# Two transformer blocks on one core: stationary width, buffers and order of products in the first attention

## The chip, the cores and the metric

One NeuronCore of a Trainium2 chip runs the whole program. The metric is the device time of one execution in microseconds, lower is better. A core has five engines with a queue each: TensorE (PE, matrix products; its weight loads are shown as PEld), VectorE (DVE), ScalarE (ACT), GpSimd (POOL) and SyncE (SP, which here issues the loads of weights).

## The reference

The input x has 512 positions of 1024 features. Two blocks are applied one after the other. What the change touches is all in the first one:

```python
proj = xn @ w_in[l]
pa, pb, pc, pd = jnp.split(proj, ...)
ya = short_conv_mixer(pa, w_sconv[l])
yb = dilated_mixer(pb, cos, sin)        # 4 heads of 64, windows with dilation
yc = forgetting_mixer(pc, b_forget[l])  # 4 heads of 64, causal, with a decay
yd = pool_mixer(pd, w_pool[l], pool_scale[l])
h = h + jnp.concatenate([ya, yb, yc, yd], axis=-1) @ w_out[l]
# memory_cross_attention: k and v of 256 memory rows
k, v = jnp.split(memn @ w_kv, 2, axis=-1)      # memn: rms_norm(mem)
```

Both mixers with heads are softmax attentions over four blocks of 128 queries. The rest (cross attention, gated feed-forward, spatial gating, differential attention, a second feed-forward) is the same before and after.

## The kernel before, in words

Activations lie as 8 chunks of 128 features x 512 positions. Each float32 operand of a large product is split into a high and a low part (ACT writes the high part, DVE subtracts it for the low one), and `product` (lines 431 to 435) issues three TensorE instructions for one: high x high, high x low, low x high. Weights come as units of 128 x 1024 floats, numbered through the program. SP loads a unit into one of two raw buffers (L398), ACT splits it (L992), DVE makes the low half (L1514), PE multiplies with it and counts it in `used`.

The stage of this case is **the first attention** (PE lines 597 to 703). It has 32 items: four groups g of two heads (group 0 and 2 dilated, 1 and 3 forgetting), and in each group four query blocks b and two heads h, so item t has group t // 8, block b = t % 8 // 2 and head h = t % 2. All engines walk through slots t = 0, 1, 2, ... in an order that is written out by hand:

- PE, slot t: `turn(t-3)` (transposes b+1 pieces of the probabilities into bank 2 or 3 of PSUM, L637), on even t `scores(t)` for both heads (L628, banks 0 and 1, 64 rows of the array each), in the first slots parts of the early output product and the gate's rows (L606), from slot 4 on `memory_half(t-4)`, and `weigh(t-5)`.
- ACT, slot t: `hi(t-4)` (high part of the turned probabilities, L1159), on t % 8 == 5 `output` (high part of the group's result, L1165), `exp(t-1)` (L1150), staging of the next group's q, k and v, `memory_out(t-4)`, with the split of a unit (L992) on even slots.
- DVE, slot t: `output`, `least(t)` (scores plus bias, and their minimum, L1742), `probs(t-2)` (L1749, L1751), `lo(t-4)` (L1757), staging (L1717, L1718), `memory_out(t-4)` (L1535 takes a key panel out of PSUM), and the low half of the unit (L1514).

`weigh(t)` multiplies the values with the turned probabilities: b+1 products, 3(b+1) instructions, with a stationary tile of 128 value columns, which are those of both heads; only the 64 rows of PSUM that belong to head h are used. The turned probabilities lie in two buffers (t % 2), so `hi(t)` waits for `weigh(t-2)`. The first `weigh` of a group waits until `output` has emptied banks 4 and 5 (semaphore mix_ready).

```python
if t % 8 == 0:
    pe.wait_ge(a1["v_staged"], t // 8 + 1)
    pe.wait_ge(early["added"], ADDED["w_out_early"] + KC)
    pe.wait_ge(mix_ready, 4 + t // 8)
...
def hi(t):
    act.wait_ge(a1["turned"], t + 1)
    if t >= 2:
        act.wait_ge(a1["pv"], t - 1)
```

`memory_half(t)` (lines 654 to 689) fills the waiting time: 16 units, each in two halves. Units m = 0 to 7 are key panels (24 instructions of 256 moving columns, into bank 6 or 7 by turns), units 8 to 15 are values (12 instructions of 512 columns), where a half takes one chunk k and both blocks of 128 memory rows, block 0 in bank 6 and block 1 in bank 7. After the first unit three column sums of squares go to bank 7 (L685, L687); ACT takes their root (L1179, L1180), DVE the reciprocals (L1778, L1779). Unit 1, which writes bank 7, waits for that root; unit 8 waits until both banks are empty of keys, unit 12 until ACT has taken block 0 of the values out of bank 6 (L1189).

After slot 36 the output product `into_residual("w_out", ...)` (L705) follows; its first column needs all eight chunks of the mixers' result (mix_ready 8).

## Time and profile before

| | us |
|---|---|
| median of 3 runs | 1979.04 (1977.53 to 1979.81) |
| time of the profiled execution | 1979.54 |
| its span, first to last instruction | 1977.7 |
| outside the span | 1.8 |
| the first attention, on the scale of the span | 141 to 285 |

The profile is of one execution. A row of a timeline gives the start and length of an instruction, its line, what it writes and reads, and in brackets how long its engine was idle before it and what ended that. PE's instructions overlap: what one costs in a full queue is the distance from its start to the next one's start, not its length. PEclk is the share of 2.4 GHz that was granted to TensorE, so 0.50 is 1.2 GHz.

### The profile page before, as it was taken

The numbers are of one execution on the slowest core, as the hardware profiler recorded it, in microseconds if no ns is written. First come the engines' busy times: TensorE is split into PE (matmuls) and PEld (weight loads), VectorE is DVE, ScalarE is ACT, GpSimd is POOL, SyncE is SP. The second block draws the span as 40 slices with busy tenths as digits, with TensorE's granted clock in tenths as the row PEclk, the third lists the DMA queues.
The fourth block names the chain that finished last, engine by engine and source line by source line (L and its number), as shares of the span: only waits on it lengthen the run. The fifth ranks groups of instructions, "written<-read, shape, count | busy, mean of one in ns | idle before, by whom it ended". The sixth has DMA issues, their size and how long they took to land.

```text
span 1977.7 us, 25235 instructions
## 1 busy us (share of the span) xinstructions
PE 1918.4 (97%) x8818; PEld 1565.4 (79%) x8818; DVE 1079.7 (55%) x1547; ACT 766.2 (39%) x1175; POOL 259.7 (13%) x206
## 2 busy tenths in 40 slices
PE   8998899899999999999999999999998999999998
PEld 6877778788787888888888888887775588888886
DVE  5866657567676624656644442255774364444323
ACT  4235455345545413453423232144554243323212
POOL 4702221020000001300100000023551020000001
PEclk9999999999999999998999999999996799999998
DMA  4222222122222322222222223222110122222222
GB/s 173 96 96 75 73 77 86 43 85 96 95 95 95 118 95 96 95 86 64 96 95 95 95 95 100 99 98 89 61 53 22 33 96 95 95 95 95 98 98 80
DMA packets 62331, 174.47 MB, mean 88 GB/s; under 512 B 5432, under 2 KB 23992, under 8 KB 62144
## 3 DMA queue, kind: packets, MB, share of 16 engines
q1 hardware_dynamic: 60912, 169.50, 25.5%
q10 hardware_dynamic: 1024, 2.94, 0.4%
q0 software_dynamic: 336, 1.25, 0.2%
q8 instruction: 37, 0.61, 0.1%
q14 instruction: 22, 0.18, 0.0%
HBM read 171.57 MB, written 2.10 MB: 88 GB/s over the span
## 4 chain that ended last, share of the span: by engine, by line
PE 91%; DVE 4%; ACT 2%; issue 1%; POOL 1%; DMA 1%; SPq 0%; DVEq 0%; ACTq 0%; POOLq 0%
PE ps L433 29%; PE ps L434 28%; PE ps L435 28%; PE ps L894 1%; PE ps L956 1%; PE ps L905 1%; POOL square_sum L2216 1%; DVE at_e L2148 1%; DMA w_raw<-in_weights 1%; DVE w_lo L1514 0%; PE ps L637 0%; PE ps L943 0%; PE ps L628 0%; DVE at_e L2132 0%; ACT w_hi L992 0%
## 5 line engine op out<-in xcount | busy, mean ns | idle before, releaser
L1514 DVE TENSOR_TENSOR w_lo<-w_raw,w_hi 128x1024 fp32r<-128x1024 f32 x302 | 379.3, 1256 | 494.5 <-ACT w_hi L992 494.1
L433 PE MATMUL ps<-xg_hi,w_hi 128*128 128x512 f32 (+1 forms) x1448 | 565.8, 391 | 13.9 <-DVE w_lo L1514 10.1
L434 PE MATMUL ps<-xg_lo,w_hi 128*128 128x512 f32 (+1 forms) x1448 | 558.9, 386 | 0.0
L435 PE MATMUL ps<-xg_hi,w_lo 128*128 128x512 f32 (+1 forms) x1448 | 558.7, 386 | 0.0
L992 ACT ACTIVATE w_hi<-w_raw 128x1024 fp32r<-128x1024 f32 x302 | 318.0, 1053 | 558.6 <-PE ps L435 553.0
L433 PEld LDWEIGHTS ps<-xg_hi,w_hi 128*128 128x128 f32 x1448 | 273.7, 189 | 80.3 <-DVE w_lo L1514 17.1
L435 PEld LDWEIGHTS ps<-xg_hi,w_lo 128*128 128x128 f32 x1448 | 273.6, 189 | 54.8
L434 PEld LDWEIGHTS ps<-xg_lo,w_hi 128*128 128x128 f32 x1448 | 273.8, 189 | 53.6 <-issue 1.0
L433 PE MATMUL ps<-hid_hi,w_hi 128*128 (+1 forms) x528 | 205.5, 389 | 0.0
L434 PE MATMUL ps<-hid_lo,w_hi 128*128 (+1 forms) x528 | 205.4, 389 | 0.0
L435 PE MATMUL ps<-hid_hi,w_lo 128*128 (+1 forms) x528 | 205.4, 389 | 0.0
L2213 POOL COPY square_sum<-squares 128x512 f32<-128x512 f32 x7 | 4.8, 689 | 1010.5 <-ACT squares L1007 1003.0
L433 PEld LDWEIGHTS ps<-hid_hi,w_hi 128*128 128x128 f32 x528 | 99.1, 188 | 20.9 <-DVE w_lo L1514 0.4
L435 PEld LDWEIGHTS ps<-hid_hi,w_lo 128*128 128x128 f32 x528 | 99.1, 188 | 20.7
L434 PEld LDWEIGHTS ps<-hid_lo,w_hi 128*128 128x128 f32 x528 | 99.1, 188 | 20.4
L2216 POOL TENSOR_TENSOR square_sum<-square_sum,squares 128x512 f32<-128x512 f32 x49 | 78.3, 1598 | 61.3 <-ACT squares L1007 60.3
L433 PE MATMUL ps<-w_hi,xg_hi 128*128 128x512 f32 x192 | 78.6, 409 | 3.4 <-DVE xa_k L1535 1.9
L435 PE MATMUL ps<-w_hi,xg_lo 128*128 128x512 f32 x192 | 76.0, 396 | 0.0
L434 PE MATMUL ps<-w_lo,xg_hi 128*128 128x512 f32 x192 | 76.0, 396 | 0.0
L1535 DVE TENSOR_TENSOR conv_a<-ps,r_cols 128x512 f32<-128x512 f32 x44 | 30.4, 691 | 78.5 <-PE ps L435 78.5
L1390 ACT ACTIVATE gate<-conv_g 128x512 f32<-128x512 f32 x44 | 27.8, 632 | 109.1 <-DVE conv_g L1535 109.1
L1520 DVE SCALAR_TENSOR_TENSOR xg_lo<-x,par,xg_hi 128x512 fp32r<-128x512 f32 x56 | 60.7, 1099 | 7.0 <-ACT xg_hi L1057 7.0
(323 smaller groups left out, 2599.2 us busy)
## 6 DMA issues: line engine op xcount, KB each, us to landing
w_raw<-in_weights SPq DMA_DIRECT2D x315, 512.0 KB, 3.2
out_cols<-result SPq DMA_DIRECT2D x8, 256.0 KB, 2.2
x<-in_x_cols SPq DMA_DIRECT2D x2, 512.0 KB, 5.2
x<-in_x_cols SPq DMA_DIRECT2D x1, 1024.0 KB, 8.4
squares<-in_mem_cols ACTq DMA_DIRECT2D x1, 512.0 KB, 3.8
sp_w<-in_spatial ACTq DMA_DIRECT2D x1, 512.0 KB, 4.1
sp_b<-in_spatial_bias ACTq DMA_DIRECT2D x1, 512.0 KB, 5.0
dil<-in_dil_table POOLq DMA_DIRECT2D x1, 448.0 KB, 9.3
```

The costliest lines, as they stand in the source:

```text
L433: nc.tensor.matmul(to, wh, xh, start=start, stop=False)
L434: nc.tensor.matmul(to, wh, xl, start=False, stop=False)
L435: return nc.tensor.matmul(to, wl, xh, start=False, stop=stop)
L894: mm = nc.tensor.matmul(ps[:, 2 * (n % 2) + h, 0:w], q_[rows, block_], k_[rows, 0:w], start=k == 0, stop=k == 2)
L905: mm = nc.tensor.transpose(ps[:, 4 + n % 2, j * P:(j + 1) * P], at3["e"][:, 2 * (n % DIFF_SLOTS), j * P:(j + 1) * P], ident)
L956: nc.tensor.matmul(ps[:, h % 4, :], pick, da["rms"], start=True, stop=True).then_inc(a3["spread"], 1)
L992: nc.scalar.activation(w_hi[:, u % 2, :], w_raw[:, u % 2, :], ACT.Copy).then_inc(w_hi_ready, 1)
L1390: nc.scalar.activation(ffn["gate"][:], ffn["tg"][:], ACT.Silu).then_inc(st["gated"], 1)
L1514: nc.vector.tensor_tensor(w_lo[:, u % 2, :], w_raw[:, u % 2, :], w_hi[:, u % 2, :].bitcast(F32), ALU.subtract).then_inc(w_ready, 1)
L1520: nc.vector.scalar_tensor_tensor(out=xg_lo[:, c, :], in0=x[:, c, :], scalar=column(gain, c), in1=xg_hi[:, c, :].bitcast(F32), op0=ALU.mult ...
L1535: return nc.vector.tensor_tensor(to, ps[:, bank, 0:cols], r_cols[:] if r is None else r, ALU.mult).then_inc(signal, 1)
L2216: nc.gpsimd.tensor_tensor(sums[:], sums[:], squares[:, c % 2, :], ALU.add).then_inc(summed, 1)
```

## The change

In the first attention alone:

- `weigh` takes only the 64 value columns of its own head as stationary columns, and both heads write rows 0 to 63 of their bank (4 or 5). ACT and DVE `output` read these rows and write the head's rows of the result. DVE's two parts each wait for ACT's part of the same head, where both waited for the second.
- Four buffers hold turned probabilities: the two of before and two more in memory that is free at that time. `hi(t)` now waits for `weigh(t-4)`.
- PE does no `weigh` in the slots with (t-5) % 8 of 0 and 1; on t % 8 == 7 it does three, items t-7, t-6 and t-5.
- DVE does `lo(t-4)` first in a slot, ahead of `output`, `least` and `probs`.
- The memory's sums of squares go to bank 5; `weigh(1)` waits for the root in place of unit 1, and PE waits ahead of the sums until the early output sums have left bank 5.
- The halves of value units are by block: the first half does both chunks k for block 0 (bank 6), the second for block 1 (bank 7). Unit 8's first half waits for 7 key panels, its second for 8; unit 12's halves wait for one block of values each; ACT takes block 0 out after the first half of the unit before.

```diff
--- before.py
+++ after.py
@@ -230,8 +230,7 @@
 
 
         at1 = dict(e=sb("at1_e", [P, 3, S], F32, m_ctx), least=sb("at1_least", [P, 3], F32, m_ctx),
-                   sums=sb("at1_sums", [P, 3], F32, m_ctx), inv=sb("at1_inv", [P, 3], F32, m_ctx),
-                   pt_hi=xg_hi[:, 4:6, :], pt_lo=xg_lo[:, 4:6, :])
+                   sums=sb("at1_sums", [P, 3], F32, m_ctx), inv=sb("at1_inv", [P, 3], F32, m_ctx))
         sb("at1_to_line", [P, LINE // 4], F32, m_ctx)
         for set_ in range(2):
             for part in ("qhi", "qlo", "khi", "klo"):
@@ -239,6 +238,14 @@
             at1[f"vhi{set_}"] = xg_hi[:, 6 + set_, :]
             at1[f"vlo{set_}"] = xg_lo[:, 6 + set_, :]
         m_ctx.close()
+
+        def turned_probs(t):
+
+            if t // 2 % 2 == 0:
+                return xg_hi[:, 4 + t % 2, :], xg_lo[:, 4 + t % 2, :]
+            if t // 8 < 2 * GC - 1:
+                return mix["hi"][:, KC - 2 + t % 2, :], mix["lo"][:, KC - 2 + t % 2, :]
+            return (at1["khi0"], at1["klo0"]) if t % 2 else (at1["qhi0"], at1["qlo0"])
 
         def mem_split(to, c):
 
@@ -339,7 +346,7 @@
                    "turned", "pt_hi", "pt", "pv", "out", "bias", "sq", "summed", "rms", "spread", "normed", "out_hi",
                    "out_lo")
         lams = stage("lambda", "dots", "exps", "done")
-        mem = stage("mem", "hi", "lo", "sq", "summed", "sums", "rms", "r", "k_ready", "v_ready")
+        mem = stage("mem", "hi", "lo", "sq", "summed", "sums", "rms", "r", "k_ready", "values", "v_ready")
         xqs = stage("xq", "ready")
         ffn_stages = {"up": stage("up", "scaled", "tapped", "steps", "gated", "product", "hid_hi", "hid", "zero"),
                       "gu": stage("gu", "scaled", "gated", "product", "hid_hi", "hid")}
@@ -640,15 +647,19 @@
             def weigh(t):
                 b, h = t % 8 // 2, t % 2
                 pe.wait_ge(a1["pt"], t + 1)
+                if t == 1:
+                    pe.wait_ge(mem["rms"], 2)
                 if t % 8 == 0:
                     pe.wait_ge(a1["v_staged"], t // 8 + 1)
                     pe.wait_ge(early["added"], ADDED["w_out_early"] + KC)
                     pe.wait_ge(mix_ready, 4 + t // 8)
                 vh, vl = group_buffers(t, ("vhi", "vlo"))
+                turned_hi, turned_lo = turned_probs(t)
                 for j in range(b + 1):
                     cols = slice(j * P, (j + 1) * P)
-                    mm = product(ps[:, 4 + h, b * P:(b + 1) * P], vh[:, cols], vl[:, cols],
-                                 at1["pt_hi"][:, t % 2, cols], at1["pt_lo"][:, t % 2, cols], j == 0, j == b)
+                    own = slice(j * P + HD * h, j * P + HD * h + HD)
+                    mm = product(ps[0:HD, 4 + h, b * P:(b + 1) * P], vh[:, own], vl[:, own],
+                                 turned_hi[:, cols], turned_lo[:, cols], j == 0, j == b)
                 mm.then_inc(a1["pv"], 1)
 
             def memory_half(t):
@@ -659,32 +670,32 @@
                     if m == 0:
                         pe.wait_ge(mem["lo"], KC)
                         pe.wait_ge(gate["rows"], 1 + N_FORGET)
-                    if m == 1:
-                        pe.wait_ge(mem["rms"], 2)
                     if 2 <= m < KC:
                         pe.wait_ge(mem["k_ready"], m - 1)
-                    if m == KC:
-                        pe.wait_ge(mem["k_ready"], KC)
-                    if m == KC + 4:
-                        pe.wait_ge(mem["v_ready"], MB)
+                if m == KC:
+                    pe.wait_ge(mem["k_ready"], KC - 1 + half)
+                if m == KC + 4:
+                    pe.wait_ge(mem["v_ready"], 1 + half)
                 if m < KC:
                     for k in range(KC // 2 * half, KC // 2 * (half + 1)):
                         wh, wl = tile(u % 2, k)
                         mm = product(ps[:, 6 + m % 2, 0:M], wh, wl, mem_split(xg_hi, k), mem_split(xg_lo, k), k == 0, k == KC - 1)
                 else:
-                    k = 2 * (m % 4) + half
-                    cols = slice(half * S, (half + 1) * S)
-                    for b in range(MB):
-                        block_ = slice(b * P, (b + 1) * P)
-                        mm = product(ps[:, 6 + b, :], mem_split(xg_hi, k)[:, block_], mem_split(xg_lo, k)[:, block_],
+                    block_ = slice(half * P, (half + 1) * P)
+                    for k in (2 * (m % 4), 2 * (m % 4) + 1):
+                        cols = slice(k % 2 * S, (k % 2 + 1) * S)
+                        mm = product(ps[:, 6 + half, :], mem_split(xg_hi, k)[:, block_], mem_split(xg_lo, k)[:, block_],
                                      w_hi[:, u % 2, cols], w_lo[:, u % 2, cols], k == 0, k == KC - 1)
                 if half:
                     mm.then_inc(used, 1)
+                elif m in (KC + 3, KC + 7):
+                    mm.then_inc(mem["values"], 1)
                 if t == 1:
                     pe.wait_ge(mem["summed"], KC)
-                    nc.tensor.matmul(ps[:, 7, 0:M], ones, memory["acc"][:], start=True, stop=True)
+                    pe.wait_ge(early["added"], ADDED["w_out_early"] + KC)
+                    nc.tensor.matmul(ps[:, 5, 0:M], ones, memory["acc"][:], start=True, stop=True)
                     for b in range(MB):
-                        mm = nc.tensor.matmul(ps[:, 7, M + b:M + b + 1], memory["acc"][:, b * P:(b + 1) * P], ones[:, 0:1],
+                        mm = nc.tensor.matmul(ps[:, 5, M + b:M + b + 1], memory["acc"][:, b * P:(b + 1) * P], ones[:, 0:1],
                                               start=True, stop=True)
                     mm.then_inc(mem["sums"], 1)
 
@@ -699,7 +710,10 @@
                     early_unit(t + 1)
                 if 0 <= t - MEM_LAG < 4 * KC:
                     memory_half(t - MEM_LAG)
-                if t >= 5:
+                if t >= 5 and (t - 5) % 8 >= 2:
+                    if t % 8 == 7:
+                        weigh(t - 7)
+                        weigh(t - 6)
                     weigh(t - 5)
 
             into_residual("w_out", KC, 0, mix["hi"], mix["lo"], mix_ready, lambda k: k + 1,
@@ -1153,16 +1167,16 @@
 
             def hi(t):
                 act.wait_ge(a1["turned"], t + 1)
-                if t >= 2:
-                    act.wait_ge(a1["pv"], t - 1)
+                if t >= 4:
+                    act.wait_ge(a1["pv"], t - 3)
                 w = P * (t % 8 // 2 + 1)
-                nc.scalar.activation(at1["pt_hi"][:, t % 2, 0:w], ps[:, 2 + t % 2, 0:w], ACT.Copy).then_inc(a1["pt_hi"], 1)
+                nc.scalar.activation(turned_probs(t)[0][:, 0:w], ps[:, 2 + t % 2, 0:w], ACT.Copy).then_inc(a1["pt_hi"], 1)
 
             def output(g):
                 act.wait_ge(a1["pv"], 8 * (g + 1))
                 for h in range(2):
                     rows = slice(HD * h, HD * h + HD)
-                    nc.scalar.activation(mix["hi"][rows, 4 + g, :], ps[rows, 4 + h, :], ACT.Copy).then_inc(a1["out_hi"], 1)
+                    nc.scalar.activation(mix["hi"][rows, 4 + g, :], ps[0:HD, 4 + h, :], ACT.Copy).then_inc(a1["out_hi"], 1)
 
             def memory_in(c):
                 if c == 0:
@@ -1176,16 +1190,19 @@
 
                 if t == 2:
                     act.wait_ge(mem["sums"], 1)
-                    nc.scalar.activation(memory["rms"][:], ps[:, 7, 0:M], ACT.Sqrt, bias=column("eps"), scale=1.0 / D).then_inc(mem["rms"], 1)
-                    nc.scalar.activation(memory["rms_rows"][:], ps[:, 7, M:M + MB], ACT.Sqrt, bias=column("eps"),
+                    nc.scalar.activation(memory["rms"][:], ps[:, 5, 0:M], ACT.Sqrt, bias=column("eps"), scale=1.0 / D).then_inc(mem["rms"], 1)
+                    nc.scalar.activation(memory["rms_rows"][:], ps[:, 5, M:M + MB], ACT.Sqrt, bias=column("eps"),
                                          scale=1.0 / D).then_inc(mem["rms"], 1)
                 m = t // 2 - 1
                 if t % 2 == 0 and 0 <= m < 2 * KC:
                     if m in (KC + 3, KC + 7):
                         h = (m - KC) // 4
-                        act.wait_ge(used, FIRST["mem_k"] + m + 1)
                         act.wait_ge(mem["r"], 2)
                         for b in range(MB):
+                            if b == 0:
+                                act.wait_ge(mem["values"], h + 1)
+                            else:
+                                act.wait_ge(used, FIRST["mem_k"] + m + 1)
                             nc.scalar.activation(xa["v"][:, b, h * S:(h + 1) * S], ps[:, 6 + b, :], ACT.Copy,
                                                  scale=memory["r_rows"][:, b:b + 1]).then_inc(mem["v_ready"], 1)
                     split(FIRST["mem_k"] + m + 2)
@@ -1754,14 +1771,15 @@
             def lo(t):
                 w = P * (t % 8 // 2 + 1)
                 dve.wait_ge(a1["pt_hi"], t + 1)
-                nc.vector.tensor_tensor(at1["pt_lo"][:, t % 2, 0:w], ps[:, 2 + t % 2, 0:w],
-                                        at1["pt_hi"][:, t % 2, 0:w].bitcast(F32), ALU.subtract).then_inc(a1["pt"], 1)
+                turned_hi, turned_lo = turned_probs(t)
+                nc.vector.tensor_tensor(turned_lo[:, 0:w], ps[:, 2 + t % 2, 0:w], turned_hi[:, 0:w].bitcast(F32),
+                                        ALU.subtract).then_inc(a1["pt"], 1)
 
             def output(g):
-                dve.wait_ge(a1["out_hi"], 2 * g + 2)
                 for h in range(2):
+                    dve.wait_ge(a1["out_hi"], 2 * g + h + 1)
                     rows = slice(HD * h, HD * h + HD)
-                    ins = nc.vector.tensor_tensor(mix["lo"][rows, 4 + g, :], ps[rows, 4 + h, :], mix["hi"][rows, 4 + g, :].bitcast(F32),
+                    ins = nc.vector.tensor_tensor(mix["lo"][rows, 4 + g, :], ps[0:HD, 4 + h, :], mix["hi"][rows, 4 + g, :].bitcast(F32),
                                                   ALU.subtract)
                 ins.then_inc(mix_ready, 1)
 
@@ -1790,14 +1808,14 @@
             for j in range(2):
                 early_sum("w_out_early", j, MIX_EARLY_BANKS[j])
             for t in range(MIX_ITEMS + 6):
+                if 0 <= t - 4 < MIX_ITEMS:
+                    lo(t - 4)
                 if t % 8 == 5 and t > 8:
                     output(t // 8 - 1)
                 if t < MIX_ITEMS:
                     least(t)
                 if 0 <= t - 2 < MIX_ITEMS:
                     probs(t - 2)
-                if 0 <= t - 4 < MIX_ITEMS:
-                    lo(t - 4)
                 g = t // 8 + 1
                 if t % 8 == 1 and g < 2 * GC:
                     stage_qk(g)
```

## Rows read from the trace of the kernel before

**Rows 1.** The page: the chain that ended last, its shares by engine.

```profile
PE 91%; DVE 4%; ACT 2%; issue 1%; POOL 1%; DMA 1%; SPq 0%; DVEq 0%; ACTq 0%; POOLq 0%
```

**Rows 2.** Windows: length, busy time of PE, PEld, DVE, ACT, POOL, PEclk, DMA share, GB/s.

```profile
182.10:199.40 17.30, 17.30 (x151) 16.39 (x150) 12.72 (x33) 9.02 (x22) 7.64 (x10) 1.00 0.20 67
...
226.50:233.30 6.80, 6.80 (x24) 5.54 (x22) 1.58 (x3) 2.05 (x5) 0.00 (x0) 0.50 0.24 77
...
264.00:267.50 3.50, 3.50 (x13) 2.89 (x12) 2.66 (x6) 0.09 (x1) 0.00 (x0) 0.51 0.00 0
...
141.00:285.00 144.00, 128.02 (x804) 107.42 (x803) 92.20 (x223) 74.74 (x162) 32.40 (x40) 0.94 0.23 75
```

**Rows 3.** Timeline, PE alone: start, length, instruction, idle time before it and who ended it.

```profile
176.30 0.55 PE L433 MATMUL ps<-xg_hi,w_hi 128*128 128x256 f32 x1 [2.53 <-ACT mem_rms_rows L1180]
...
202.49 0.30 PE L433 MATMUL ps<-xg_hi 128*128 128x128 f32 x1 [1.36 <-DVE mix_lo L1764]
...
203.75 0.41 PE L637 MATMUL ps<-con,at_e 128*128 128x128 f32 x2 [0.74 <-DVE xg_lo L1757]
...
210.47 0.52 PE L637 MATMUL ps<-con,at_e 128*128 128x128 f32 x3 [0.96 <-DVE xg_lo L1757]
...
225.74 0.47 PE L433 MATMUL ps<-w_hi,xg_hi 128*128 128x512 f32 x1 [1.88 <-DVE xa_k L1535]
...
255.60 0.47 PE L433 MATMUL ps<-w_hi,xg_hi 128*128 128x512 f32 x1 [1.30 <-ACT xa_v L1189]
...
284.62 0.50 PE L433 MATMUL ps<-mix_hi,w_hi 128*128 128x512 f32 x1 [0.57 <-DVE mix_lo L1764]
```

**Rows 4.** Timeline, PE: inside a weighing at the granted clock 1.00, then in one at 0.50.

```profile
185.58 0.22 PE L433 MATMUL ps<-xg_hi 128*128 128x128 f32 x1
185.64 0.28 PE L434 MATMUL ps<-xg_lo,xg_hi 128*128 128x128 f32 x1
185.76 0.27 PE L435 MATMUL ps<-xg_hi,xg_lo 128*128 128x128 f32 x1
...
179.11 0.41 PE L434 MATMUL ps<-xg_lo,xg_hi 128*128 128x128 f32 x1
179.32 0.41 PE L435 MATMUL ps<-xg_hi,xg_lo 128*128 128x128 f32 x1
```

**Rows 5.** Groups of weight loads over the span, 128 and 8 columns: mean ns behind the comma.

```profile
L453 PEld LDWEIGHTS ps<-square_sum,con 128*128 128x128 f32 x14 | 2.6, 188 | 1.5 <-issue 1.0
...
L943 PEld LDWEIGHTS ps<-squares,con 128*8 128x8 f32 x16 | 0.9, 88 | 2.9 <-ACT squares L1485 1.6 <-issue 0.9
```

**Rows 6.** Timeline, PE, differential attention: weighing, two products with 8 stationary columns, weighing.

```profile
1529.33 0.27 PE L435 MATMUL ps<-at_pt_hi,at_v_lo 128*128 128x128 f32 x1
1529.53 1.02 PE L943 MATMUL ps<-squares,con 128*8 128x512 f32 x2
1530.49 0.33 PE L433 MATMUL ps<-at_pt_hi,at_v_hi 128*128 128x128 f32 x1
1530.65 0.27 PE L434 MATMUL ps<-at_pt_lo,at_v_hi 128*128 128x128 f32 x1
```

**Rows 7.** Timelines of ACT, DVE and PE around the memory's root.

```profile
174.23 1.28 ACT L1179 ACT_TABLE_LOAD   x1
...
176.19 1.75 DVE L1778 RECIPROCAL mem_r_cols<-mem_rms 128x256 f32<-128x256 f32 x1
...
180.43 0.69 DVE L1742 CUSTOM_DVE_ANT_0 at_e<-ps,dil 128x512 f32<-128x512 f32 x1 [0.88 <-PE ps L637]
...
183.11 0.52 PE L637 MATMUL ps<-con,at_e 128*128 128x128 f32 x3
```

**Rows 8.** Timelines of ACT and of DVE at the first change of group.

```profile
199.72 1.20 ACT L1165 ACTIVATE mix_hi<-ps 64x512 fp32r<-64x512 f32 x2
...
200.96 1.39 DVE L1764 TENSOR_TENSOR mix_lo<-ps,mix_hi 64x512 fp32r<-64x512 f32 x2 [1.25 <-ACT mix_hi L1165]
...
205.23 0.69 DVE L1742 CUSTOM_DVE_ANT_0 at_e<-ps,proj 128x512 f32<-128x512 f32 x1 [1.62 <-PE ps L628]
```

## The prediction

> **What bounds the kernel now.** I read the chain that ended last first: TensorE is 91% of it [rows 1], so an edit pays only where it shortens PE's own work or a wait of PE. Then windows over the first attention [rows 2]: of 144.0 us between 141 and 285 PE is busy 128.0, so about 16 us are waits. Within a group it doesn't wait at all (17.30 of 17.30 us from 182.1 on), while the granted clock falls to 0.50 from 226.5 to 233.3, to 0.51 in 264.0 to 267.5, and once more after 175. Last, the waits one by one in PE's timeline [rows 3]. Seven are to be seen: 2.53 us for the memory's root, three at the first change of group (1.36, 0.74, 0.96), 1.88 for the eighth key panel, 1.30 for the first half of the values, 0.57 ahead of the output product. The other two changes of group repeat the pattern of the first (0.03, 0.74, 0.68 and 1.43, 0.74). That is 13 us; the other 3 lie in the first slots and stay. The stage is bound by PE inside a group, and by the ACT-DVE chain at its seams and at the memory's root. About 0.2% (4 us) is what a measurement of this kernel can tell from no change.
>
> **Part 1, narrow weighing.** There are 240 instructions, in 32 blocks of n = 3, 6, 9, 12. A full-width one costs 0.12 to 0.11 us from start to start; the one whose load had been done in advance cost 0.06 (185.58 to 185.64) [rows 4]. So 128 moving columns need 0.06, and the load of 128 stationary columns sets the pace. Loads take 188 ns at 128 columns and 88 at 8, that is 0.83 ns a column [rows 5]; 64 columns fewer save 0.053. The pace inside a block should fall from 0.112 to 0.065, by 0.047 for each of its n-1 further instructions.
>
> Against that stands the change of width. Before shows none at 64 columns; the nearest rows are the products with 8 columns between weighings [rows 6]. Going in, the interval is 0.20 in place of 0.11: 0.09 more. Coming out, the second interval is 0.16 (1530.49 to 1530.65) in place of 0.11, 0.05 more, and the first I price like the way in, 0.09. The first narrow product, whose successor's load can't be done ahead, takes 0.11 in place of 0.06: 0.05. Together a block pays 0.09 + 0.05 + 0.09 + 0.05 = 0.28 (0.29 unrounded), and its gain is 0.047(n-1) - 0.29: -0.19, -0.05, 0.09, 0.23 for the four sizes. The first three blocks of a group are now one of 12 instructions: 0.35 + 11 x 0.065 = 1.06, against 3 x 0.06 + 9 x 0.112 = 1.19, so 0.13. A group saves 0.13 - 0.05 + 2 x 0.09 + 2 x 0.23 = 0.72, four save 2.9; some 0.4 falls where DVE sets the pace: **2.5 us**. Bounds: if a change of width costs nothing, 208 x 0.047 = 9.8, some 8 of it where PE sets the pace; if loads don't get shorter and the switch stays, 24 x 0.29 = -7. I take the middle, since both prices have a row of the same kind.
>
> The Trainium skill ("TensorEngine Tiling (Array Packing)", Key Properties) says that a change of tiling mode drains TensorE. The trace agrees (0.20 in place of 0.11 where the width changes), and the page gives no price. The skill ("TensorE: Matmul & The Clock Gate", Back-to-back issue gap) gives about 81 ns for sustained pairs of load and product at 128 columns. The trace has 112 at full width and differs; with 81 as the narrow pace, by that page alone, this part would come to about -0.6 us.
>
> **Part 2, sums in bank 5.** PE loses its 2.53 us wait, but what is late next is DVE. The sums end at 172.2. ACT no longer waits for `weigh(0)` with `hi(2)`, so its table load of 1.28 [rows 7] starts then, at 172.25 instead of 174.23, and the root is there at 174.1. DVE is the late one. It was free for the reciprocal at 176.1; scores(6), for which it waited before that, come 0.36 earlier (3 x 0.12, as `weigh(0)` is gone from ahead of them), and `lo(2)` (0.34) is done before, so it is free at 175.4. The reciprocal (1.75, at 176.19 before) starts 0.8 earlier. The key panel and the unit's low half follow, then least(7), which had waited 0.88 for PE at the low clock: 180.43 - 0.8 - 0.88 = 178.75, plus lo(3) 0.34 = 179.1. least (0.69) and probs (0.5) follow and turn(5) starts at about 180.5, where it was 183.11: **2.6 us**, the low clock of that place included. PE has turn(4) at 175.2, half a unit (12 x 0.12) and the three weighings (1.1) until then, gets there at 178 and stands for 2.5 us: nearly the same wait, at another instruction. The added wait for early sums is covered, since PE at that point has already waited for DVE's later slot 4. `weigh(1)`'s wait for the root finds it done (174.1 against 177).
>
> **Part 3, value units by block.** Unit 8's first half needs the seventh panel only, out two slots earlier: the 1.88 goes. Its second half comes a slot later and finds the eighth done, which was so by 225.7 even then. Unit 12's first half still waits for ACT's copy of block 0. DVE and ACT reach this place when they did, so half of the 1.30 is my estimate of what stays, between none and all. **2.5 us.** ACT could take block 0 earlier, but it stands behind exp in its queue, so I count no more.
>
> **Part 4, four buffers, weighing put off, `lo` first.** At a change of group count from R = 199.55, when weigh(7) is done (0.17 ahead of ACT's first copy; `hi(9)` lies between). Before, turn(11) starts at R+4.2 and turn(13) at R+10.9 [rows 3]. ACT's two copies take 1.20 and DVE's two subtractions 1.39, starting after the second copy (200.96) [rows 8]. Now `hi(9)` is out of the way, DVE starts after the first copy, at R+0.63, and `lo` doesn't stand behind least and probs: turn(11) at about R+3.3. PE has only half a unit to do there (1.5 us) and waits 1.7: the 1.36 turns up again at turn(11). From least(14) to turn(13) it was 5.24 (205.23 to 210.47); with lo(10) ahead of it, 4.9. least(14) starts 1.48 behind turn(11), so turn(13) starts at R+9.7, with weighings 8 to 10 done as before: 1.2 us. The second change gives 1.0; at the third, without staging behind it, 0.5. **2.7 us**, not the 6.7 that the waits add up to. `hi(8g+12)` now waits for the first of the three weighings; hi, lo and turn behind it have a slot of time. The last output gives **0.6** [rows 3]: DVE's first subtraction runs beside ACT's second copy.
>
> **Part 5, the clock.** A weighing instruction takes 0.21 at 0.50 against 0.11 [rows 4]. In 226.5 to R2 = 230.5, the end of weigh(15) and PE-bound, that cost 1.8 (12 x 0.1 for it and 3 x 0.2 for products of 512 columns); after 264.0, 1.6. The first of these follows the 1.88 wait, which goes, the second a wait that is moved. Both back: **3.4**. But waits of 2.5 and three times 1.7 stand in the new order, as long as those after which the clock fell, and some will be followed by a low stretch. One of 6.8 us costs 6.8 x (1 - 0.112/0.213) = 3.2; I charge one, **-3.0**.
>
> **Sum**: 2.5 + 2.6 + 2.5 + 2.7 + 0.6 + 3.4 - 3.0 = 11.3. The profiled execution took 1979.5 (span 1977.7 and 1.8 around it), so 1968.2; the median of the runs is 0.5 below it: 1967.7. Behind the stage nothing changes, and the weight stream has room (DMA share 0.23 over the stage) [rows 2].
>
> **The rivals.**
> - *The forecast*, gain 7 to 15: 0.48.
> - *Cheap switches, no low clock*: 14.3 + (8 - 2.5) = 19.8, so 1959.2. For it: 64 columns is not 8, and the products of 8 columns are of another kind. Against: the waits that stay. Gains over 15: 0.21.
> - *Waits moved and the clock falls at two or three seams*: 14.3 - 3 x 3.2 = 4.7, so 1974.3. For it: the seams keep 1.7 us waits. Against: the first change of group had 1.36 and 0.96 and the clock stayed. Gains of 4 to 7: 0.17.
> - *The narrowing doesn't do what it says* (loads not shorter, switch in full): 11.3 - 2.5 - 7 = 1.8, so 1977.2, within 0.2%: 0.08.
> - *Slower*: half-width products leave TensorE looking idle, and the clock stays low in the weighing slots through the stage. Each 6.8 us stretch costs 3.2, so past the 14.3 it takes five, and from six of them (41 of the 100 us) it is over 1979.0 by 5: 1984. For it: the stage's granted clock is 0.94 even now [rows 2]. Against: weighing is 240 instructions of over 800, and full-width units stand in every slot. 0.06.
>
> Faster 0.86, same 0.08, slower 0.06. The range takes the price of the switch from near zero to full, and no to three low stretches: 1959.5 to 1975.
>
> **What would show it.** Weighing groups of 80 instructions with 64 columns at some 0.065 start to start, and 0.20 at the first of a block (part 1). No wait at unit 1, but some 2.5 us at turn(5) for DVE (part 2); no wait at unit 8, 0.6 at unit 12 (part 3); waits of 1.7 at turn(11), (19), (27) on DVE in place of the weighing's (part 4); one low stretch in the stage. It would be wrong if these waits are gone or longer, if the pace inside a block stays 0.11, or if the clock is low throughout.

## The result, and the profile after

The changed kernel takes 1957.11 us (median of four runs, 1956.26 to 1957.49) against 1979.42 for the one before (1977.53 to 1982.03): ratio 0.9886, interval 0.9869 to 0.9903. It is 22.3 us faster. The sign was forecast, the size was not: 11.3 us were, and the time lies below the range.

The profiled execution took 1957.36, with a span of 1955.5. I measure the stage from the first scores to the first product of the cross attention's queries. That is 163.03 us before (141.44 to 304.47) and 145.45 after, so **17.6 us are gained in the stage and 5.2 behind it**, in work that is the same instruction by instruction. Ahead of the stage 0.6 are lost: the first scores start at 142.06 instead of 141.44. Windows of both kernels, columns as in [rows 2]. Of the changed kernel: the stage, the rest, two stretches of low clock in the stage (a third begins at 166.7) and the longest one behind it. Below them, of the kernel before: the stage, the rest and the longest stretch. All three stretches of low clock in the stage come to 13.65 us after, and to 17.07 before.

```profile
142.06:287.51 145.45, 133.59 (x888) 109.38 (x888) 108.40 (x238) 86.88 (x179) 42.33 (x46) 0.95 0.25 82
287.51:1955.50 1667.99, 1634.97 (x7375) 1333.24 (x7373) 876.58 (x1202) 633.42 (x938) 158.90 (x110) 0.98 0.26 87
...
180.30:187.10 6.80, 6.12 (x32) 5.67 (x33) 3.94 (x12) 3.67 (x8) 2.20 (x2) 0.50 0.31 110
248.60:252.00 3.40, 3.40 (x12) 2.27 (x12) 1.64 (x5) 1.82 (x4) 0.87 (x2) 0.50 0.00 0
1474.00:1504.72 30.72, 24.32 (x100) 18.03 (x100) 17.11 (x52) 15.92 (x43) 6.47 (x5) 0.50 0.06 18
```

```profile
141.44:304.47 163.03, 147.05 (x887) 123.44 (x887) 106.79 (x238) 86.01 (x179) 41.03 (x46) 0.95 0.22 74
304.47:1977.70 1673.23, 1639.95 (x7375) 1336.77 (x7373) 876.45 (x1202) 633.33 (x938) 159.06 (x110) 0.97 0.26 86
1492.80:1526.93 34.13, 28.35 (x112) 20.25 (x112) 16.93 (x53) 16.66 (x45) 5.87 (x5) 0.50 0.05 16
```

PE was busy 147.05 us in the stage and is now 133.59, for the same number of instructions; the waits over 0.3 us fell less, from 15.9 to 11.8. So what went is mostly busy time of PE, less work and less low clock together. In the rest, 7375 instructions on both sides, 1673.23 became 1667.99, and the clock is the only thing that differs: the low stretch of the differential attention is 34.13 long before and 30.72 after, and the two after it, at 1540.6 and 1963.9, are shorter by 3.3 to 3.4 too.

The waits, in PE's timeline after, answer to [rows 3]:

```profile
180.98 0.90 PE L644 MATMUL ps<-con,at_e 128*128 128x128 f32 x3 [2.65 <-DVE at_e L1768]
...
201.25 0.44 PE L644 MATMUL ps<-con,at_e 128*128 128x128 f32 x2 [1.79 <-DVE at_e L1768]
...
207.59 0.55 PE L644 MATMUL ps<-con,at_e 128*128 128x128 f32 x3 [0.85 <-DVE at_e L1768]
...
224.80 0.44 PE L644 MATMUL ps<-con,at_e 128*128 128x128 f32 x2 [1.54 <-DVE at_e L1768]
...
248.17 0.44 PE L644 MATMUL ps<-con,at_e 128*128 128x128 f32 x2 [1.86 <-DVE at_e L1768]
...
267.63 0.50 PE L440 MATMUL ps<-mix_hi,w_hi 128*128 128x512 f32 x1 [0.70 <-DVE mix_lo L1782]
```

They stand where the prediction put them: 2.65 at turn(5), 1.79, 1.54 and 1.86 at turn(11), (19) and (27), all on DVE's probs (L1768); none at units 1, 8 and 12. Weigh(7) ends at 197.79 and ACT's first copy starts at 197.83. Set against that start, turn(11) comes at +3.4 and turn(13) at +9.8; forecast were +3.3 and +9.7.

What wasn't where it was put is the weighing. PE's timeline after: two rows of a block at the granted clock 0.50 (185.38), then a block of nine at 1.00 with the product ahead of it and the one behind it. Below it is the group of one of its weight loads:

```profile
185.38 0.31 PE L440 MATMUL ps<-mix_hi,xg_hi 128*64 128x128 f32 x1
185.48 0.31 PE L441 MATMUL ps<-mix_lo,xg_hi 128*64 128x128 f32 x1
...
188.34 0.28 PE L442 MATMUL ps<-xg_hi,w_lo 128*128 128x256 f32 x1
188.46 0.22 PE L440 MATMUL ps<-xg_hi 128*64 128x128 f32 x1
188.52 0.22 PE L441 MATMUL ps<-xg_lo,xg_hi 128*64 128x128 f32 x1
188.58 0.22 PE L442 MATMUL ps<-xg_hi,xg_lo 128*64 128x128 f32 x1
...
188.94 0.22 PE L442 MATMUL ps<-xg_hi,xg_lo 128*64 128x128 f32 x1
189.00 0.40 PE L644 MATMUL ps<-con,at_e 128*128 128x128 f32 x2
```

```profile
L442 PEld LDWEIGHTS ps<-xg_hi,xg_lo 128*64 128x64 f32 x32 | 4.3, 135 | 0.0
```

Inside a block the distance is 0.060, against 0.112 at full width [rows 4] (0.10 against 0.21 at the low clock). **Going in, it is 0.12 (188.34 to 188.46), what a product of 256 columns takes in front of its own kind; coming out, 0.06.** A change of width costs nothing here. Over all blocks behind a product of 256 columns, at the full clock, the interval going in is 0.117 to 0.122, and was 0.117 to 0.120 at full width; from the first transpose of a turn to its second it is 0.136, and was 0.134 (medians).

### The profile page after: what moved, and what is told of

The parts are those of the page before. It is cut to its first block, busy times and chain, and to the rows that moved or that the text cites. A ratio compares the mean times of both kernels' runs of the same rounds, so it can differ in the third digit from the quotient of the medians.

```text
span 1955.5 us, 25234 instructions
## 1 busy us (share of the span) xinstructions
PE 1899.1 (97%) x8818; PEld 1546.8 (79%) x8818; DVE 1081.4 (55%) x1547; ACT 767.2 (39%) x1175; POOL 260.8 (13%) x206
## 4 chain that ended last, share of the span: by engine, by line
PE 90%; DVE 5%; ACT 2%; issue 1%; POOL 1%; DMA 1%; SPq 0%; POOLq 0%; DVEq 0%; ACTq 0%
PE ps L440 29%; PE ps L441 28%; PE ps L442 28%; PE ps L908 1%; DVE w_lo L1531 1%; PE ps L970 1%; PE ps L919 1%; POOL square_sum L2234 1%; DMA w_raw<-in_weights 1%; DVE at_e L2166 1%; ACT w_hi L1006 0%; PE ps L635 0%; PE ps L644 0%; DVE at_e L1759 0%; PE ps L957 0%
## 5 line engine op out<-in xcount | busy, mean ns | idle before, releaser
L440 PE MATMUL ps<-xg_hi,w_hi 128*128 128x512 f32 (+1 forms) x1448 | 565.8, 391 | 12.6 <-DVE w_lo L1531 11.3
```

Of the source, the lines that this page charges most:

```text
L440: nc.tensor.matmul(to, wh, xh, start=start, stop=False)
```

## The experiments

Runs e1 to e12 stand each against the kernel before on the same chip; e1 to e4 share nine runs of it (1979.06, 1977.25 to 1983.29), e5 to e8 seven (1978.43, 1973.16 to 1981.35), e9 to e12 eleven (1977.22, 1973.43 to 1982.06). The changed kernel itself ran with another set, beside 1979.42. So a difference between one of these runs and the changed kernel is across sets, whose medians of the kernel before lie up to 2.2 us apart, and one of 1 or 2 us proves nothing by itself.

### e1 and e2: narrowing alone, and everything but it

e1 is the kernel before with the narrow `weigh` (and `output` reading rows 0 to 63); e2 is the changed kernel without both. The main lines of e2's edit:

```diff
-    mm = product(ps[0:HD, 4 + h, b * P:(b + 1) * P], vh[:, own], vl[:, own],
+    mm = product(ps[:, 4 + h, b * P:(b + 1) * P], vh[:, cols], vl[:, cols],
```

> The kernel before with the narrow weighing alone (64 stationary columns, rows 0 to 63 of the bank); two buffers, order, banks and halves as before. Theory A, the change of width costs nothing between 128 and 64 columns: the pace in a block is 0.06 and so is the first interval, 32 blocks save 208 x 0.05 = 10.6 us of PE time, some 8 to 10 of it in the time, about 1970, with the seven waits of before in place. Theory B, the one on record, a switch of 0.29 a block: 32 x 0.29 = 9.3 against 9.8, so no gain at all, about 1979.

> The changed kernel with 128 stationary columns again in the weighing, all else as changed. Theory A: slower than the changed kernel by 8 to 10 us, about 1966. Theory B: slower by 2.5, about 1960. The waits at turn(5), turn(11), turn(19), turn(27) stay at 2.6 and 1.5 to 1.9 either way.

e1: 1969.38 (1967.33 to 1976.04), ratio 0.9954, interval 0.9938 to 0.9969, 9.7 us faster than before. e2: 1963.51 (1962.12 to 1964.22), ratio 0.9919, 0.9902 to 0.9936, 6.4 slower than the changed kernel. So e1 is as its theory A had it (about 1970), and e2 lies between its theories (2.5 and 8 to 10 slower), nearer to A. The stage of e1, that of e2, and that of the changed kernel in a second profile (e15, below):

```profile
141.37:293.31 151.94, 131.41 (x887) 106.94 (x887) 106.25 (x238) 85.76 (x179) 40.90 (x46) 0.99 0.24 79
```

```profile
141.63:292.52 150.89, 142.05 (x887) 119.11 (x887) 108.77 (x238) 88.04 (x179) 42.35 (x46) 0.98 0.24 80
```

```profile
141.87:285.54 143.67, 131.01 (x888) 107.10 (x887) 108.41 (x238) 86.70 (x179) 42.37 (x46) 0.98 0.26 84
```

Narrowing was priced at 2.5 us, with 9.8 as its upper bound if a change of width is free. The stages differ by 11.1 us without the rest of the change (151.94 against 163.03) and by 5.4 with it (145.45 against 150.89), the times by 9.7 and 6.4. All are more than 2.5. The work alone is 208 x 0.052 = 10.8 us, at the full clock, and in both pairs part of it is waited for: PE's waits over 0.3 us grow from 15.9 to 19.7, and from 8.6 to 11.8.

What sets 11.1 and 5.4 apart is the clock, which these two comparisons don't hold equal. The stage has 17.07 us at the granted clock 0.50 in the kernel before and 3.41 in e1, but 6.83 in e2 and 13.65 in the changed kernel. In e15 the changed kernel has 6.83, as e2 has, and by its stage narrowing gives 7.2 (150.89 less 143.67). In e1, 13.66 us less of low clock are worth up to 7 of the 11.1 (an estimate: an instruction takes twice as long at 0.50). Whether narrowing itself makes the low stretches fewer isn't shown. **So narrowing gives more than was forecast, 5.4 to 7.2 us beside the rest of the change.**

### e3, e4 and e11: 32, 96 and 8 columns

The changed kernel with another width. 32 and 8 leave out values, 96 takes columns of the other head.

```diff
-    own = slice(j * P + HD * h, j * P + HD * h + HD)
-    mm = product(ps[0:HD, 4 + h, b * P:(b + 1) * P], vh[:, own], vl[:, own],
+    own = slice(j * P + HD * h, j * P + HD * h + 8)
+    mm = product(ps[0:8, 4 + h, b * P:(b + 1) * P], vh[:, own], vl[:, own],
```

> The changed kernel with 32 stationary columns in each weighing instruction; it leaves out the other 32 value columns of each head, so the attention's result is not computed in full. Theory A2, the switch costs only towards a quarter of the width (as the 8-column products showed): pace 0.06 as with 64, but 0.09 more at the first weighing of a block and some 0.15 more behind it, 24 x 0.24 = 5.8 us of PE time, 3 to 5 us slower. Theory A3, the 8-column products were slow for another reason: same time as the changed kernel.

> The changed kernel with 96 stationary columns (both heads take columns 0 to 95, so head 1 is computed wrongly). If the load sets the pace by 0.83 ns a column, the interval is 0.083 (64 columns: 0.06, 128: 0.11), so 240 x 0.023 = 5 us of PE time more, some 4 us slower. If the pace has two steps only, a full and a half width, it is 0.11 or 0.06 and the time that of the wide or of the narrow kernel.

> The changed kernel with 8 stationary columns in each weighing (most of the values are left out, to see the price of a change of width alone). Theory A (width has no price by itself; the 0.09 more at the products of 8 columns comes from what stands around them): pace about 0.06, entering interval 0.117 as with 64 and 32 columns, time 1957. Theory B (8 columns do cost a switch): 0.09 more going in and coming out, 32 blocks by 0.28, some 8 us less where DVE sets the pace: 1962 to 1966.

e3: 1957.23, ratio 0.989 (0.9874 to 0.9907); e4: 1960.92, 0.9907 (0.9891 to 0.9924); e11: 1956.95, 0.9889 (0.9864 to 0.9914). PE's timeline, from the last product ahead of the block on, in e11 and then in e4:

```profile
187.40 0.28 PE L442 MATMUL ps<-xg_hi,w_lo 128*128 128x256 f32 x1
187.52 0.22 PE L440 MATMUL ps<-xg_hi 128*8 128x128 f32 x1
187.58 0.22 PE L441 MATMUL ps<-xg_lo,xg_hi 128*8 128x128 f32 x1
187.64 0.23 PE L442 MATMUL ps<-xg_hi,xg_lo 128*8 128x128 f32 x1
```

```profile
187.68 0.28 PE L442 MATMUL ps<-xg_hi,w_lo 128*128 128x256 f32 x1
187.80 0.22 PE L440 MATMUL ps<-xg_hi 128*96 128x128 f32 x1
...
188.11 0.25 PE L441 MATMUL ps<-xg_lo,xg_hi 128*96 128x128 f32 x1
188.20 0.25 PE L442 MATMUL ps<-xg_hi,xg_lo 128*96 128x128 f32 x1
188.29 0.25 PE L440 MATMUL ps<-xg_hi 128*96 128x128 f32 x1
```

The pace is 0.06 at 8, 32 and 64 columns, 0.085 at 96 and 0.112 at 128. That was e4's first theory, and it came 3.8 us slower than the changed kernel, as forecast (some 4). From 128 to 96 it falls by 0.027, which is 0.84 ns a column, as the loads had it [rows 5]; below 64 nothing is gained, since the 128 moving columns need 0.06 anyway. The Trainium skill ("TensorE: Matmul & The Clock Gate", LDWEIGHTS) puts a load at its columns divided by 1.2, in ns. By that, an estimate, it is 107, 80 and 53 ns for 128, 96 and 64; the trace agrees within 5 ns for the first two (112 and 85) and for the third shows the 60 of the moving side.

Eight columns enter and leave like the others. So the 0.09 more at the differential attention's products of 8 columns [rows 6], on which the prediction's price hung, isn't a price of the width. Those products have 512 moving columns and other operands, and each waits for a semaphore of its own. They are of another kind too: two of them take 0.96 (1529.53 to 1530.49), where a product of 512 columns in the stage takes 0.23. The 512 columns alone don't cost it, since at two places in the stage before a weighing ahead of a product of 512 moving and 128 stationary columns takes 0.11 (from 277.56 and from 281.62 on). Which of the rest costs the 0.09 was not tried.

### e5 and e7: the bank and the buffers, each undone

e5 puts the sums back into bank 7, and unit 1 waits for the root. e7 has two turned buffers, a weighing in every slot and `hi(t)` behind `weigh(t-2)`, with `lo` first and bank 5 kept.

```diff
 # e5
-                if t == 1:
-                    pe.wait_ge(mem["rms"], 2)
...
+                    if m == 1:
+                        pe.wait_ge(mem["rms"], 2)
...
-                    nc.tensor.matmul(ps[:, 5, 0:M], ones, memory["acc"][:], start=True, stop=True)
+                    nc.tensor.matmul(ps[:, 7, 0:M], ones, memory["acc"][:], start=True, stop=True)
 # e7
-                if t >= 4:
-                    act.wait_ge(a1["pv"], t - 3)
+                if t >= 2:
+                    act.wait_ge(a1["pv"], t - 1)
...
-                if t >= 5 and (t - 5) % 8 >= 2:
-                    if t % 8 == 7:
-                        weigh(t - 7)
-                        weigh(t - 6)
+                if t >= 5:
                     weigh(t - 5)
```

> The changed kernel with the sums back in bank 7 (so that unit 1 waits for the root again); the four buffers stay. Theory A, the bank is not what brings the 2.6 us: ACT comes to its root early because hi(2) no longer waits for the first weighing, which is the buffers' work, and turn(5) hangs on DVE either way. Then turn(5) stays within 0.5 us of where it is (16.1 us after the first scores), TensorE waits about 1 us at unit 1 and that much less at turn(5), and the time is 1957 to 1958. Theory B, as the prediction had it (Part 2 is the bank's): turn(5) 2.6 us later, 1959.7. In both the clock can add or take some 3 us.

> The changed kernel with two turned buffers, a weighing in every slot and hi(t) behind weigh(t-2); lo stays ahead on DVE, sums stay in bank 5. Theory A (Part 4 as predicted, and Part 2's gain is the bank's): the weighings wait again at the three changes of group, turn(5) stays: 1959 to 1960. Theory B (the early root is the buffers' work): hi(2) stands behind the first weighing again, so the root comes about 2 us later and turn(5) with it, on top of the seams: 1961.5 to 1963.

e5: 1957.77 (1956.61 to 1957.91), ratio 0.9899 (0.988 to 0.9919). e7: 1960.44 (1958.45 to 1965.44), 0.992 (0.9895 to 0.9945). PE's timeline in e5, then in e7 (turn(5), and the first change of group):

```profile
175.40 0.36 PE L440 MATMUL ps<-xg_hi,w_hi 128*128 128x256 f32 x1 [0.58 <-ACT mem_rms_rows L1193]
...
181.63 0.55 PE L644 MATMUL ps<-con,at_e 128*128 128x128 f32 x3 [2.08 <-DVE at_e L1767]
```

```profile
181.17 0.55 PE L640 MATMUL ps<-con,at_e 128*128 128x128 f32 x3 [2.28 <-DVE at_e L1761]
...
199.91 0.24 PE L436 MATMUL ps<-xg_hi 128*64 128x128 f32 x1 [0.81 <-DVE mix_lo L1775]
...
200.88 0.44 PE L640 MATMUL ps<-con,at_e 128*128 128x128 f32 x2 [0.60 <-DVE at_e L1761]
```

In e5 unit 1 waits 0.58 for the root and turn(5) 0.58 less than in the changed kernel; turn(5) comes 38.93 after the first scores, and 38.92 in the changed kernel (the 16.1 of the expectation is counted from turn(0)). **The bank brought nothing by itself**, with four buffers in place: theory A. In e7 turn(5) comes at 39.64, with DVE's reciprocal at 34.75, where the kernel before has it too; with four buffers, with or without the bank, it is at 34.03. So the buffers (hi(2) behind no weighing, and no weighing ahead of scores(6)) give 0.7 of what Part 2 booked for the bank. The kernel before has turn(5) at 41.67, and the other 2.0 are neither the bank's nor the buffers'. e1 has neither of them, and turn(5) comes there at 39.58, held up only by DVE's lo(3):

```profile
180.95 0.52 PE L637 MATMUL ps<-con,at_e 128*128 128x128 f32 x3 [0.89 <-DVE xg_lo L1758]
```

What e1 and e7 share is the narrow weighing and no low stretch ahead of turn(5); in the kernel before one runs from 33.86 to 40.69 behind the first scores. The clock alone moves turn(5) there, to 41.73 and 40.61 in its two further profiles (e13, e14). How the 2.0 divide between clock and width was not tried.

e7's time lies between the two theories' (1959 to 1960, 1961.5 to 1963), and its four times scatter over 7 us. Its stage is 146.30, 0.85 over the changed kernel's and 2.6 over that of e15, with 10.24 us of low clock between their 13.65 and 6.83. The weighings wait 0.8 at each change of group again, but turn(11) comes at once behind (0.6 in place of 1.8).

### e6 and e12: value units by chunk again, and by block alone

```diff
-                    block_ = slice(half * P, (half + 1) * P)
-                    for k in (2 * (m % 4), 2 * (m % 4) + 1):
-                        cols = slice(k % 2 * S, (k % 2 + 1) * S)
-                        mm = product(ps[:, 6 + half, :], ...
+                    k = 2 * (m % 4) + half
+                    cols = slice(half * S, (half + 1) * S)
+                    for b in range(MB):
+                        block_ = slice(b * P, (b + 1) * P)
+                        mm = product(ps[:, 6 + b, :], ...
```

with the waits of before (e6, on the changed kernel); e12 is the reverse of it on the kernel before.

> The changed kernel with the value units halved by chunk again. Theory A (Part 3 as predicted): waits of about 1.9 at unit 8 and 1.3 at unit 12 come back, turn and scores behind them wait for nothing else, 1959.6. Theory B: with the weighings 6.4 us shorter TensorE has more room and the waits are longer than they were (over 2.5 and 2), and a low clock stretch follows them: 1961 or more. Theory C: what is waited for at these units is taken off the 1.5 us wait at the third change of group, nothing gained: 1957.5.

> The kernel before with the value units by key block alone. Theory A (Part 3 is worth 2.5 to 3 us also by itself, and the 5 us that came later than the stage belong to how long the granted clock stays low there, which follows no part): stage about 160 in place of 163, time 1975 to 1976.5; the rest behind the stage is 1673 as before or 1668, whichever, and the time follows it. Theory B (with every weighing 128 wide and two buffers, what unit 8 no longer waits for is lost at the next change of group): 1978 to 1979.

e6: 1960.78 (1958.68 to 1961.04), ratio 0.9911 (0.9891 to 0.9932), 3.7 over the changed kernel; its stage 148.23, 2.8 over.

```profile
220.87 0.48 PE L440 MATMUL ps<-w_hi,xg_hi 128*128 128x512 f32 x1 [1.68 <-DVE xa_k L1548]
...
245.83 0.48 PE L440 MATMUL ps<-w_hi,xg_hi 128*128 128x512 f32 x1 [0.42 <-ACT xa_v L1202]
```

The wait at unit 8 returns with 1.68, that at unit 12 with 0.42, and a low stretch of 3.4 us begins at 221.3, just behind the first. The low clock of the stage is 13.65 us in all, as in the changed kernel, so this difference isn't the clock's: Part 3 was sized about right (2.5).

e12: 1971.3 (1970.32 to 1977.77), ratio 0.9972 (0.9952 to 0.9992), 5.9 faster. Stage and rest, then two rows of PE's timeline (the second change of group, and unit 12):

```profile
141.72:301.37 159.65, 145.29 (x887) 122.30 (x887) 106.72 (x238) 85.98 (x179) 40.99 (x46) 0.96 0.23 75
301.37:1969.90 1668.53, 1635.39 (x7375) 1334.24 (x7373) 876.76 (x1202) 633.24 (x938) 158.96 (x110) 0.98 0.26 87
```

```profile
232.04 0.30 PE L433 MATMUL ps<-xg_hi 128*128 128x128 f32 x1 [1.42 <-DVE mix_lo L1768]
...
253.60 0.47 PE L433 MATMUL ps<-w_hi,xg_hi 128*128 128x512 f32 x1 [0.72 <-ACT xa_v L1193]
```

Its stage gained 3.4, as theory A had it, but not for theory A's reason alone. The wait of 1.88 at unit 8 is gone and that of 1.30 at unit 12 is 0.72, near the half that Part 3 let stand. In return the weighing at the second change of group waits 1.42, where it waited 0.03: that is theory B's mechanism. The waits over 0.3 us fall by 1.7 in all, and the stage has 3.41 us less of low clock, which is worth the other 1.7 (an estimate, half its length). So with two buffers and wide weighings Part 3 brings about 1.7 by itself, and 2.8 with the rest of the change. Its rest is the short one, although nothing is edited there.

### e8: `lo` behind least and probs again

```diff
-                if 0 <= t - 4 < MIX_ITEMS:
-                    lo(t - 4)
                 if t % 8 == 5 and t > 8:
                     output(t // 8 - 1)
                 if t < MIX_ITEMS:
                     least(t)
                 if 0 <= t - 2 < MIX_ITEMS:
                     probs(t - 2)
+                if 0 <= t - 4 < MIX_ITEMS:
+                    lo(t - 4)
```

> The changed kernel with DVE's lo behind least and probs again and its output first. Theory A (Part 4 as predicted: lo first is worth 0.3 to 0.7 at each change of group, since lo no longer stands behind two others when TensorE wants to weigh): 1958 to 1959. Theory B: turn(11), (19), (27) hang on probs, which comes 0.35 earlier when lo is behind it, and the weighings have slots of time with four buffers: 0 to 1 us faster than the changed kernel, 1956 to 1957.

1958.5 (1957.98 to 1961.10), ratio 0.9907 (0.9886 to 0.9928); the stage is 146.91, with 10.24 us of low clock (145.45 and 143.67 in the two profiles of the changed kernel, with 13.65 and 6.83). The time is 1.4 us over the changed kernel's, no more than the sets differ: theory A, weakly.

### e9 and e10: what the remaining waits are worth

The changed kernel's waits at turn(11), (19) and (27) are for `probs`, and on DVE that stands behind `output`, 1.37 us of subtractions:

```profile
198.77 1.37 DVE L1782 TENSOR_TENSOR mix_lo<-ps,mix_hi 64x512 fp32r<-64x512 f32 x2
200.17 0.56 DVE L1759 CUSTOM_DVE_ANT_0 at_e<-ps,proj 128x384 f32<-128x384 f32 x1
...
200.84 0.35 DVE L1768 TENSOR_SCALAR at_e<-at_e,at_inv 128x256 f32<-128x256 f32 x1
```

e9 puts `output` last in its slot. e10 does so too, and moves the reciprocals of the root and the first key panel one slot later:

```diff
-                if t % 8 == 5 and t > 8:
-                    output(t // 8 - 1)
                 if t < MIX_ITEMS:
                     least(t)
                 if 0 <= t - 2 < MIX_ITEMS:
                     probs(t - 2)
+                if t % 8 == 5 and t > 8:
+                    output(t // 8 - 1)
 # e10 also, in DVE's memory_out
-                if t == 2:
+                if t == 3:
                     dve.wait_ge(mem["rms"], 2)
...
-                if t % 2 == 0 and 0 <= m < KC:
+                if t == 3:
+                    dve.wait_ge(used, FIRST["mem_k"] + 1)
+                    scaled(xa["k"][:, 0, :], 6, mem["k_ready"], M, memory["r_cols"][:])
+                if t % 2 == 0 and 0 < m < KC:
```

> The changed kernel with DVE's output subtractions behind least and probs of their slot instead of ahead of them. Theory A (the waits of 1.8, 1.5 and 1.9 us at turn(11), (19) and (27) are there because probs stands behind the output, which waits for ACT's copies): they fall below 0.5 each, the stage is 3 to 5 us shorter, 1952.5 to 1954.5. Theory B: DVE sets the pace over the whole change of group, so the wait comes back at turn(13), (21), (29) or at the weighing that needs the bank: stage within 1 us of the changed kernel's 145.4, time 1956 to 1958.

> The kernel above, and DVE's two reciprocals of the root with the first key panel one slot later (behind least and probs of slot 5). Theory A: turn(5) then comes about 2 us earlier and TensorE's wait of 2.65 us there falls to under 1; 1950 to 1952.5. Theory B: unit 2 waits for the late first key panel in its place, nothing gained on the kernel above.

e9: 1956.59 (1953.15 to 1958.73), ratio 0.9884 (0.9866 to 0.9902). e10: **1951.49** (1949.12 to 1954.04), ratio 0.9868 (0.985 to 0.9885); its slowest run is below the changed kernel's fastest, 1956.26, though against the kernel before of its own set the ratio is less clear of the changed kernel's (0.9886, 0.9869 to 0.9903). e9's stage and rest, then e10's, and e10's turn(5) and unit 2:

```profile
143.09:283.35 140.26, 132.61 (x887) 108.52 (x887) 108.05 (x238) 86.40 (x179) 42.39 (x46) 0.96 0.26 86
283.35:1956.90 1673.55, 1640.24 (x7375) 1336.80 (x7373) 876.68 (x1202) 633.43 (x938) 158.98 (x110) 0.97 0.26 86
```

```profile
141.76:278.72 136.96, 128.76 (x887) 104.80 (x887) 107.79 (x238) 86.39 (x179) 42.37 (x46) 1.00 0.27 88
278.72:1947.30 1668.58, 1635.39 (x7375) 1333.64 (x7373) 876.73 (x1202) 633.43 (x938) 158.95 (x110) 0.98 0.26 87
```

```profile
178.54 0.55 PE L644 MATMUL ps<-con,at_e 128*128 128x128 f32 x3 [0.52 <-DVE at_e L1768]
...
180.77 0.36 PE L440 MATMUL ps<-xg_hi,w_hi 128*128 128x256 f32 x1 [1.21 <-DVE xa_k L1552]
```

In e9 the wait of 1.79 is 0.36 and those of 1.54 and 1.86 are under 0.5; the stage is 140.26, 5.2 shorter, as theory A had it; in second profiles of both it is 140.62 against 143.67, 3.1 shorter. But the time hardly moves, because in the profile the rest is the long one, 1673.55: what was won in the stage is lost behind it. In e10 turn(5) waits 0.52 in place of 2.65 and comes 2.1 earlier, as theory A had it, but unit 2 waits 1.21 for its late key panel, and the clock doesn't fall in the stage at all (1.00). The stage is 136.96 and the rest the short one. Its waits over 0.3 us sum to 8.2, no less than the 7.7 and 8.0 of e9's two profiles. What is shorter is PE's busy time, 128.76 against 132.61, by the clock. So e10's time, inside the range of theory A, doesn't show that moving the reciprocals saves a wait.

### e13 to e16: is the rest behind the stage a matter of the kernel?

The kernel before (twice), the changed one and that of e9, profiled again without an edit.

> The kernel before, unchanged, profiled again. Theory A (the 5 us behind the stage belong to the execution: where the steps of the granted clock fall): the rest behind the stage is 1668 or 1673, and the time goes with it, about 1973 to 1975 or 1978 to 1981. Theory B (they belong to the kernel): 1673 each time.

> A third profile of the kernel before, unchanged. Theory A: the rest behind the stage is 1668 or 1673, and the time goes with it. Theory B: 1673 again.

> The changed kernel, unchanged, profiled again. Theory A: the rest is 1668 or 1673, with a time of 1957 or about 1961. Theory B: 1668 and 1957.

> The kernel of e9, unchanged, profiled again. Theory A: the stage is again about 140.3, 5 us shorter than the changed kernel's, and with a rest of 1668 the time is 1952 to 1954; with a rest of 1673, 1957 to 1959. Theory B: the rest is 1673 again.

Times 1979.83, 1981.59, 1956.30 and 1957.79; rests 1673.3, 1673.6, 1669.0 and 1673.5: as theory B had it, in these four. The rest of e13, for one:

```profile
304.69:1978.00 1673.31, 1640.03 (x7375) 1336.90 (x7373) 876.30 (x1202) 633.24 (x938) 158.94 (x110) 0.97 0.26 86
```

Over all sixteen profiles of runs and the two shown first, the rest is 1673.2 to 1673.6 in the kernel before, e1 and e9, each time they were profiled, and 1667.8 to 1669.4 in all the others. It is not any part of the change that makes it short: each of bank, blocks, buffers, `lo` and width is undone in one of e2 and e5 to e8, and all of these have the short one; e12 has it with blocks alone. Nor does it go with the stage's length: 163, 152 and 140 us have the long rest, 160, 151, 144 to 148 and 137 the short one. What goes with it is where the low stretches lie. Counted from the first scores of the differential attention, the long stretch begins at 123.5 to 124.3 us where the rest is long (34.13) and at 122.9 to 123.3 where it is short (30.72). What places it wasn't found.

Four further profiles are few, and the times of the executions without a profile speak against a rule of the kernel. Of the kernel before four took 1973.2 to 1974.0 at a mean granted clock of 0.975 to 0.977, about 5 us under the others' middle. One of e9 took 1953.15 at 0.977, where its two profiled ones had 0.974 and 0.975. The other way, one of e12 took 1977.77 at 0.972 and one of e1 1976.04 at 0.971, each over 5 us above all others of its run. So the same kernel has executions with more and with less low clock; whether it lies in the stage or behind it can't be told without a profile. Between theories A and B it stays open.

## Why the prediction was wrong, point by point

- **Part 1 failed.** The step is "Against that stands the change of width": 0.29 us a block, taken from products of 8 columns. Measured is none (0.12 in and 0.06 out, at 64, 32 and 8 columns). The other half, the pace, was right in kind and came out slightly below the forecast, 0.060 for 0.065, by loads that get shorter with the columns. I called the middle between the bounds the likeliest because both prices "have a row of the same kind"; but the row of the switch was not of the same kind, it differed in moving columns and operands too. That it differed stood in the rival's own line ("64 columns is not 8") and should have had more weight. 2.5 us were forecast; 5.4 to 7.2 of the stage is what narrowing gave beside the rest, near the 8 that the prediction had as its bound for a free change of width.
- The rule that a change of tiling mode drains TensorE (the Trainium skill, "TensorEngine Tiling (Array Packing)", Key Properties) I had called borne out by the 0.20. The trace of the changed kernel doesn't bear it out: 240 instructions of 64 columns between products of 128, and no drain to be seen in their distances.
- **Part 2** was right in time (turn(5) 2.75 us earlier against the first scores, forecast 2.6; a wait of 2.65 there, forecast 2.5) and wrong in cause: by e5 the bank gave none of it, by e7 the buffers 0.7, and the other 2.0 lie between the narrow weighing and the clock. That the sum was right is in part luck.
- **Part 3**, 2.5: e6 has 2.8 of stage, e12 by itself 1.7 in waits. The half of the wait at unit 12 that I let stand is gone in the changed kernel.
- **Part 4**: the places of turn(11) and turn(13) came within 0.1 us, and the three waits within 0.2 of 1.7. Undone one at a time, buffers and `lo` cost 0.9 and 1.5 of stage against the first profile of the changed kernel, and 2.6 and 3.2 against the second; the clock differs in both, so their sizes are not measured better than that. The last output had 0.57 us of wait ahead of the output product and has 0.70 now, so its 0.6 can't be told from the rest.
- **Part 5**: two low stretches were to be given back and one charged. In the profile of the changed kernel there are three, 13.65 us in all, against 17.07 before; in its second profile two, 6.83 in all, with a stage of 143.67. With wide weighings (e2) it is 6.83 as well. In its third profile the kernel before has 23.89, with a stage of 163.87. So the length that was forecast, 13.65, is what the first profile shows, but the clock gave more than the net 0.4: 3.41 us less of it are worth about 1.7 (an estimate at twice the time per instruction), and 10.24 less, as in e2, about 5. It alone moves the stage by some 2 us from one execution to the next. That is most of why e2's stage gained 12.1 over before, where Parts 2 to 5 came to 8.8.
- **"Behind the stage nothing changes" failed as well.** The work didn't change; its clock did, for 5.2 us, and why is open. No row of before could have shown it, but the low stretches there could have been a bound: with 91 us of them behind the stage, their length is worth some us either way, and the range should have had room for that.
- In sum the stage gave 17.6 where 11.3 were forecast: 12.1 from before to e2 (forecast 8.8) and 5.4 from e2 to the changed kernel (forecast 2.5; 7.2 by the second profile). Another 5.2 came on top behind it (forecast none). The forecast missed by 11.0: 3 to 5 us by the price of the switch, 5.2 by the rest, and the remainder by the low clock in the stage. Without the 5.2 the time would have been 1962.3, inside the range. The rival of 1959.2, "cheap switches, no low clock", came nearest: its first half is what happened, its second is not. The slower rival, in which half-width products bring the clock down, is answered by e11: with 8 columns the stage has 6.83 us of low clock, as at 64 (e15) and at 128 (e2).
